# First attention layer of a four-layer transformer kernel: key tiles ahead of query tiles, square sums inside the next product, rope without GpSimd, and the first norm beside the modulation

## The chip, the cores and the metric

The kernel runs on one core of one Trainium2 chip. The metric is the device time of one execution in microseconds. The engines are called TensorE (PE in the profile), VectorE (DVE), ScalarE (ACT), GpSimd (POOL) and SyncE (SP, whose queue issues most loads). All numbers are f32.

## The reference, cut to what matters

Two blocks of two layers each work on 512 image tokens and 256 context tokens of width 1024. The change lies in layer 0, up to the first score of its attention:

```python
def rms_norm(x, g):
    y = xf * lax.rsqrt(jnp.mean(xf * xf, axis=-1, keepdims=True) + EPS)
    return (y * g.astype(jnp.float32)).astype(x.dtype)

mx = jnp.split(c_act @ ada_w[i] + ada_b[i], 6, axis=-1)   # modulation, mc from c_ctx
h_x = modulate(rms_norm(x, norm1_g[i]), mx[0], mx[1])     # h * (1 + scale) + shift
h_c = modulate(rms_norm(y_ctx, norm1_g[i]), mc[0], mc[1])
...
q_x, k_x, v_x = jnp.split(h_x @ w_qkv, [qd, qd + kvd], axis=-1)   # 16 q heads, 4 kv heads of 64
q_x = rope_2d(rms_norm(q_x.reshape(B, S, N_HEADS, HEAD_DIM), q_gain), tables)
k_x = rope_2d(rms_norm(k_x.reshape(B, S, N_KV_HEADS, HEAD_DIM), k_gain), tables)
k_c = rms_norm(k_c.reshape(B, L, N_KV_HEADS, HEAD_DIM), k_gain)
...
s_ctx = einsum(qb, k_c) * scale; s_loc = einsum(qb, kb) * scale   # then softmax and values
```

The other layers (feed-forward, retention, two layers with four mixers each) are computed by code that the change leaves as it is.

## The kernel before

**Tiling.** Activations lie transposed: 8 tiles of 128 features by T = 768 tokens (512 image, 256 context). Every f32 factor of a large product is split into a high part (fp32r) and a low part, the rest. A weight unit of 128x1024 is loaded into `WR`; ScalarE rounds it to `WH` (`refill`, L692) and VectorE subtracts to get `WL` (L1037). There are two buffers each, so unit u waits until product u-2 is over. `product` (L313 to L328) makes one output tile of 128 features: 8 input tiles times three products (WH with HH, WH with HL, WL with HH). `product_pair` makes two output tiles at once as the input tiles become ready.

**Order.** Each engine has a program written out by hand; `on(name, event)` is a semaphore wait, `on.up` its increment. No scheduler moves anything, so the code is the order of each engine.

**Start.** The modulation of layer 0 is twelve parts of 512 columns. A part is two loads of 1 MB (`ada`), eight small matmuls (`ada_sum`, L363) into PSUM, a ScalarE copy (`ada_copy`, L698) and a turn into columns (`ada_turn`, L370). Parts 0 to 3 come ahead of the first norm, through two buffers `AR0`. Then the squares of X are made on ScalarE in two buffers (`all_squares`, L708) and summed over the features by eight products with a matrix of 1/1024 (`mean_square`, L388). Then come root (L703, L705), two Newton steps (`newton`, L1082, L1083), and for each tile: a scaling on VectorE (L1108, L1111), scale and shift on ScalarE (L725 to L732), and the low part on VectorE (L1095, L1098).

**Query, key and value tiles.** `attention` makes 8 query tiles, then 2 key tiles, then the value rows. A tile goes through: product into PS[0] or PS[1]; raw copy and square on ScalarE (L785, L786); square sum over each head's 64 features on TensorE (L438); root and Newton steps; the gain (L1181); the rope on VectorE (half swap L1183, sine multiply L1184, addition L1191) with the cosine multiply on GpSimd (L1542), which writes into the square's buffer. TensorE's order is product n, modulation part 4+n, square sum n, turn, product n+1. A key tile is then split into high and low parts and copied to the other half of the partitions (`aK`, L806, L807, L1203, L1204), from one buffer `aKF`. The value rows (`product_rows`, L352) go to six PSUM banks and from there to `aV`. Last come mask loads, the stacking of the first block's queries (`stack`, L820, L1222) and the first score (L459).

## Time and profile before

| | us |
|---|---|
| three executions, median | 3689.19 |
| three executions, lowest and highest | 3688.1, 3695.85 |
| the profiled execution, in all | 3685.29 |
| its span from first to last instruction | 3684.0 |
| TensorE busy | 3449.4 (94%) |
| VectorE busy | 1743.7 (47%) |
| ScalarE busy | 1214.7 (33%) |
| GpSimd busy | 255.6 (7%) |
| mean granted clock of TensorE | 0.963 |
| first matmul of the product pair | 63.61 |
| first score of the attention | 235.49 |

A time in the profile is counted from the span's start. A row of the timeline gives start, length, engine, source line, operation, output and inputs; in brackets is how long the engine was idle before it and what it then got. The granted clock is a share of 2.4 GHz: 0.50 is 1.2 GHz.

### The profile page before, as it was taken

The numbers are of one execution on the slowest core, as the hardware profiler recorded it, in microseconds if no ns is written. First come the engines' busy times: TensorE is split into PE (matmuls) and PEld (weight loads), VectorE is DVE, ScalarE is ACT, GpSimd is POOL, SyncE is SP. The second block draws the span as 40 slices with busy tenths as digits, with TensorE's granted clock in tenths as the row PEclk, the third lists the DMA queues.
The fourth block names the chain that finished last, engine by engine and source line by source line (L and its number), as shares of the span: only waits on it lengthen the run. The fifth ranks groups of instructions, "written<-read, shape, count | busy, mean of one in ns | idle before, by whom it ended". The sixth has DMA issues, their size and how long they took to land.

```text
span 3684.0 us, 42824 instructions
## 1 busy us (share of the span) xinstructions
PE 3449.4 (94%) x17952; PEld 2782.0 (76%) x17952; DVE 1743.7 (47%) x2627; ACT 1214.7 (33%) x1696; POOL 255.6 (7%) x337
## 2 busy tenths in 40 slices
PE   6979989999989999998999999889999989979998
PEld 3767778888865756656888786578888878568886
DVE  3567454333343333426757425546535433644343
ACT  4357442112232221224222424442212233543232
POOL 0101100000100000001001100010000010010001
PEclk7989999999999999999999998899999999889999
DMA  5400033323221211113544210023323322012222
GB/s 204 182 26 2 30 115 126 120 92 126 82 69 35 94 48 58 65 41 139 192 149 173 98 58 29 12 87 127 133 84 126 105 86 81 12 46 97 97 97 86
DMA packets 87776, 334.24 MB, mean 91 GB/s; under 512 B 11168, under 2 KB 14240, under 8 KB 83744
## 3 DMA queue, kind: packets, MB, share of 16 engines
q1 hardware_dynamic: 66416, 252.85, 19.3%
q0 software_dynamic: 21168, 78.65, 6.4%
q8 instruction: 142, 2.33, 0.2%
q14 instruction: 50, 0.41, 0.0%
HBM read 329.37 MB, written 2.10 MB: 90 GB/s over the span
## 4 chain that ended last, share of the span: by engine, by line
PE 89%; DVE 4%; ACT 4%; issue 1%; DMA 1%; SPq 0%; POOL 0%; DVEq 0%; ACTq 0%
PE PS L326 65%; PE PS L352 6%; PE PS L548 3%; PE PS L521 2%; PE PS L339 2%; PE PS L620 1%; PE PS L470 1%; PE PS L513 1%; PE PS L483 1%; PE PS L645 1%; PE PS L459 1%; PE PS L591 1%; DMA AR<-in_ada 1%; PE PS L632 1%; DVE dP L1450 1%
## 5 line engine op out<-in xcount | busy, mean ns | idle before, releaser
L692 ACT ACTIVATE WH<-WR 128x1024 fp32r<-128x1024 f32 (+1 forms) x376 | 419.0, 1115 | 1686.8 <-PE PS L326 1448.1
L326 PE MATMUL PS<-HH,WH 128*128 128x512 f32 (+1 forms) x3120 | 944.5, 358 | 29.7 <-DVE HL L1427 11.0
L326 PE MATMUL PS<-HL,WH 128*128 128x512 f32 (+1 forms) x3120 | 936.9, 355 | 0.0
L326 PE MATMUL PS<-HH,WL 128*128 128x512 f32 (+1 forms) x3120 | 936.6, 355 | 0.0
L1037 DVE TENSOR_TENSOR WL<-WR,WH 128x1024 fp32r<-128x1024 f32 (+1 forms) x376 | 486.0, 1293 | 928.6 <-ACT WH L692 928.2
L326 PEld LDWEIGHTS PS<-HH,WH 128*128 128x128 f32 x3120 | 514.6, 189 | 122.4 <-issue 16.6
L326 PEld LDWEIGHTS PS<-HL,WH 128*128 128x128 f32 x3120 | 514.4, 189 | 88.0 <-issue 2.2
L326 PEld LDWEIGHTS PS<-HH,WL 128*128 128x128 f32 x3120 | 513.9, 189 | 86.6
L326 PE MATMUL PS<-DH,WL 128*128 128x512 f32 (+1 forms) x1056 | 318.7, 356 | 0.0
L326 PE MATMUL PS<-DL,WH 128*128 128x512 f32 (+1 forms) x1056 | 318.7, 356 | 0.0
L326 PE MATMUL PS<-DH,WH 128*128 128x512 f32 (+1 forms) x1056 | 318.6, 356 | 0.0
L1163 DVE SCALAR_TENSOR_TENSOR X<-PS,MOD,X 128x512 f32<-128x512 f32 x96 | 60.6, 659 | 368.0 <-PE PS L326 368.0
L326 PEld LDWEIGHTS PS<-DL,WH 128*128 128x128 f32 x1056 | 174.2, 188 | 30.0
L326 PEld LDWEIGHTS PS<-DH,WL 128*128 128x128 f32 x1056 | 174.2, 188 | 30.0
L326 PEld LDWEIGHTS PS<-DH,WH 128*128 128x128 f32 x1056 | 174.1, 188 | 30.0
L1068 DVE SCALAR_TENSOR_TENSOR PS<-AT,CB 128x1024 f32<-128x1024 f32 x144 | 176.5, 1226 | 0.0
L352 PE MATMUL PS<-WH,HH 128*128 128x256 f32 (+1 forms) x416 | 142.2, 342 | 27.5 <-DVE HL L1095 15.8
L1536 POOL DMA_DIRECT2D AT<-in_adat x144 | 76.0, 528 | 1149.5 <-DVE AT L1068 574.7
L352 PE MATMUL PS<-WL,HH 128*128 128x256 f32 (+1 forms) x416 | 141.0, 339 | 0.0
L352 PE MATMUL PS<-WH,HL 128*128 128x256 f32 (+1 forms) x416 | 141.0, 339 | 0.0
L1528 POOL TENSOR_TENSOR WK<-WK,WK 128x768 f32<-128x768 f32 (+1 forms) x56 | 116.9, 2087 | 329.3 <-ACT WK L708 328.8
L767 ACT ACTIVATE DH<-WK 128x768 fp32r<-128x768 f32 (+1 forms) x88 | 65.1, 739 | 185.4 <-DVE WK L1154 185.4
(258 smaller groups left out, 3707.1 us busy)
## 6 DMA issues: line engine op xcount, KB each, us to landing
WR<-in_win SPq DMA_DIRECT2D x176, 512.0 KB, 3.5
AT<-in_adat POOLq DMA_DIRECT2D x144, 512.0 KB, 3.8
WR<-in_wdn SPq DMA_DIRECT2D x64, 704.0 KB, 4.0
WR<-in_wret SPq DMA_DIRECT2D x64, 512.0 KB, 3.6
WR<-in_zin SPq DMA_DIRECT2D x36, 512.0 KB, 3.5
AR<-in_ada SPq DMA_DIRECT2D x8, 1024.0 KB, 4.9
aV<-in_ada SPq DMA_DIRECT2D x8, 1024.0 KB, 4.9
aAR<-in_ada SPq DMA_DIRECT2D x8, 1024.0 KB, 6.5
```

Source lines behind the costliest of these rows:

```text
L326: mm = PE.matmul(dst[:, a:b], w[u % 2][:, k * P:(k + 1) * P], h[:, k, a:b], start=(k == 0 and i == 0), stop=(k == nk - 1 and i == 2))
L339: mm = PE.matmul(dst[v][:, a:b], w[(u + v) % 2][:, k * P:(k + 1) * P], h[:, k, a:b], start=(k == 0 and i == 0), stop=(k == KT - 1 and i == 2))
L352: mm = PE.matmul(dst(m), h[:, k0 + k, m * P:(m + 1) * P], w[u % 2][:, k * width:(k + 1) * width], start=(first and k == 0 and i == 0 and n ...
L521: mm = PE.matmul(d, M.rV[:, m, e * P:(e + 1) * P], M.rAT[:, m, :], start=(m == 0), stop=(m == 5))
L548: mm = PE.matmul(PS[half][:, 512 * v:512 * v + 512], wt[half][:, col:col + P], y[:, k, :], start=(k == 0 and i == 0), stop=(k == 3 and i = ...
L692: AC.activation(M.WH[u % 2][:, 0:n], M.WR[u % 2][:, 0:n], COPY).then_inc(*on.up("w_hi", u))
L767: AC.activation(M.DH[:, j, 0:n], HF[:, 0:n], COPY).then_inc(*on.up("d_hi", (l, jj)))
L1037: VE.tensor_tensor(M.WL[u % 2][:, 0:n], M.WR[u % 2][:, 0:n], M.WH[u % 2][:, 0:n].bitcast(F32), ALU.subtract).then_inc(*on.up("w_lo", u))
L1068: i = VE.scalar_tensor_tensor((PS[3], M.AT[v % 3])[j][:, :], M.AT[v % 3][:, :], 1.0, M.CB[:, j, :], ALU.mult, ALU.mult, accum_out=MOD[:, l ...
L1163: i = VE.scalar_tensor_tensor(X[:, m, a:b], PS[m % 2 if m else 2][:, a:b], MOD[:, l, 40 + m, j:j + 1], X[:, m, a:b], ALU.mult, ALU.add)
L1528: PO.tensor_tensor(WK[2][:, 0:n], WK[2][:, 0:n], WK[k % 2][:, 0:n], ALU.add).then_inc(*on.up("square_summed", (tag, k)))
L1536: PO.dma_start(M.AT[v % 3][:, :], dram["adat"][l - 1, v]).then_inc(*on.up(f"mod_load{v % 3}", (l, v), 16))
```

## The change

- **Start.** `AR0` has four buffers, so parts 2 and 3 wait for the sums two parts back. ScalarE squares X between the copies of the modulation parts. GpSimd adds up seven of the eight squares (`squares`, the helper the later norms use); TensorE's mean square is two products and stands after the turn of part 2, ahead of part 3. VectorE does root, Newton steps and five scalings and then the modulation of parts 0 to 3 and the low parts of the first two weight units. The first tile of this norm takes the path of the others.
- **Order of tiles.** `QK = (8, 9, 0, ..., 7)`: keys first. The weight array is laid out in that order. The keys' rope result stands in the places of queries 6 and 7 until it is split, which happens after the tiles at places 3 and 4.
- **Inside the next product.** `product` calls `between(k)` ahead of each input tile. From place 2 on, the square sum of the tile before stands ahead of input tile 2 (3 in one case) and the turn ahead of input tile 5; the last one's stand inside the value rows.
- **ScalarE** takes the square of a tile after the Newton steps of the tile before.
- **Rope.** The cosine multiply is on VectorE, in place, and GpSimd has no part in it.
- **Values.** The rows go to three banks, two tiles to a bank; ScalarE copies a whole bank and VectorE none. The mask loads wait for the last rope, and `stack` comes before the last weight units.

```diff
 def first_ada(self):
-        self.AR0 = [t(f"AR0{i}", [P, 4, 512]) for i in range(2)]
+        self.AR0 = []
+        for i, at in enumerate(FIRST_ADA):
+            self.top = at
+            self.AR0.append(self.tile(f"AR0{i}", [P, 4, 512]))
...
+QK = (8, 9, 0, 1, 2, 3, 4, 5, 6, 7)
+V_PLACES = (0, 1, 2)
...
         for k in range(nk):
-            if between and k == 3:
-                between()
+            if between:
+                between(k)
...
     def attention():
         u = FIRST["qkv"]
-        for n in range(10):
-            half = n % 2
-            if n == 0:
-                product_pair(u, PS, ALL, ("h_lo", "0a"))
-            if n > 1:
-                product(u + n, PS[half], (HH, HL), KT, ALL, ("q_squared", n - 2))
-            if n < 8:
-                ada_sum(0, A0 + n, buf, (0, A0 + n - 1))
-            PE.wait_ge(*on("q_squared", n))
-            PE.wait_ge(*on("table", "attention") if n == 0 else on("rms", ("q", n - 1)))
+        def square_sum(p):
+            PE.wait_ge(*on("q_squared", QK[p]))
+            PE.wait_ge(*on("rms", ("q", QK[p - 1])) if p else on("table", "attention"))
...
+        def beside(p, at, squares_at, turn_at):
+            if at == squares_at and p != 1:
+                square_sum(p)
+            if at == turn_at and p > 1:
+                ada_turn(0, A0 + QK[p], M.aKF)
+        product_pair(u, PS, ALL, ("h_lo", "0a"))
+        for p in range(2, 10):
+            last = p - 1 if p > 2 else 0
+            product(u + p, PS[p % 2], (HH, HL), KT, ALL, ("q_squared", QK[p - 2]) if p > 3 else None, None,
+                    lambda k: beside(last, k, 3 if p == 3 else 2, 5))
+            if p == 2:
+                square_sum(1)
+            ada_sum(0, A0 + QK[p], buf, (0, A0 + QK[p] - 1))
...
     for nb in range(A0):
-        ada_sum(0, nb, M.AR0, before_part(0, nb))
+        ada_sum(0, nb, M.AR0[2 * (nb % 2):2 * (nb % 2) + 2], before_part(0, nb))
         ada_turn(0, nb, M.EV0)
-    mean_square("0a", ALL, False)
+        if nb == A0 - 2:
+            mean_square("0a", ALL)
...
-    for nb in range(A0):
-        ada_copy(0, nb, M.EV0[:, :])
+    ada_copy(0, 0, M.EV0[:, :])
+    AC.wait_ge(*on("x_load", 0))
+    squares("0a", T, range(4))
+    ada_copy(0, 1, M.EV0[:, :])
+    squares("0a", T, range(4, KT))
+    ada_copy(0, 2, M.EV0[:, :])
+    root("0a", T)
+    ada_copy(0, 3, M.EV0[:, :])
     refill(0)
     refill(1)
-    AC.wait_ge(*on("ada_turned", (0, A0 - 1)))
-    AC.wait_ge(*on("x_load", 0))
-    all_squares("0a", T)
     norm("0a", 0, 0, ALL)
...
+            if p:
+                AC.wait_ge(*on("rms", ("q", QK[p - 1])))
+            AC.activation(M.aSQ[:, :], PS[p % 2][:, 0:T], SQUARE).then_inc(*on.up("q_squared", n))
+            refill(u + p + 2)
...
+            if p in (3, 4):
+                key_high(p - 3)
...
+        AC.wait_ge(*on("rope", QK[-1]))
         for g in range(2):
             stack(0, g)
+        for v in range(2):
+            refill(u + 12 + v)
+        for i in range(3):
+            AC.wait_ge(*(on("v_rows", i) if i < 2 else on("product", u + 11)))
+            a = (2, 4, 0)[i]
+            AC.activation(flat(M.aV, a, a + 2), bank(PS, V_PLACES[i]), COPY).then_inc(*on.up("aV", i))
...
+            VE.tensor_tensor(raw[:, 0:S], raw[:, 0:S], M.aCOS[:, :], ALU.mult)
             step(VE.tensor_tensor(M.aT2[:, :], M.aT2[:, :], M.aSIN[:, :], ALU.mult), ("q_sin", n))
-            VE.wait_ge(*on("q_t1", n))
...
-        PO.wait_ge(*on("table", "attention"))
-        for n in range(10):
-            PO.wait_ge(*on("q_normed", n))
-            PO.tensor_tensor(M.aSQ[:, 0:S], M.aRAW[n % 2][:, 0:S], M.aCOS[:, :], ALU.mult).then_inc(*on.up("q_t1", n))
...
     for nb in range(1, A0):
         for half in range(2):
-            ada(0, nb, half, buf, (0, nb - 1))
+            ada(0, nb, half, buf[2 * (nb % 2):2 * (nb % 2) + 2], (0, nb - 2) if nb > 1 else None)
```

How TensorE's order moves in the start, in the kernel before, from the sum of part 3 (`AR`, `CAC`) to the mean squares (`WK`, `ONE`):

```order
L363 MATMUL PS<-AR_71,CAC 32x512 x4
L363 MATMUL PS<-AR_72,CAC 32x512 x4
L370 MATMUL PS<-SEL,EV_73 128x2 x4
L388 MATMUL PS<-WK_103,ONE 128x512
L388 MATMUL PS<-WK_103,ONE 128x256
L388 MATMUL PS<-WK_104,ONE 128x512
L388 MATMUL PS<-WK_104,ONE 128x256
```

And in the changed kernel, from the sum of part 2 to the product pair:

```order
L381 MATMUL PS<-AR_71,CAC 32x512 x4
L381 MATMUL PS<-AR_72,CAC 32x512 x4
L388 MATMUL PS<-SEL,EV_75 128x2 x4
L399 MATMUL PS<-WK_107,ONE 128x512
L399 MATMUL PS<-WK_107,ONE 128x256
L399 MATMUL PS<-WK_106,ONE 128x512
L399 MATMUL PS<-WK_106,ONE 128x256
L381 MATMUL PS<-AR_73,CAC 32x512 x4
L381 MATMUL PS<-AR_74,CAC 32x512 x4
L388 MATMUL PS<-SEL,EV_75 128x2 x4
L353 MATMUL PS<-HH,WH_55 128x512
```

The mean square has become two products (the sum `WK_107` and the last square `WK_106`) and stands ahead of part 3 instead of behind it.

TensorE after the product pair, before: the pair's last matmuls, then one modulation part (`aV`, `aAR`), the square sum of tile 0 (`aBD`) and the turn (`SEL`). The same five follow once more for tile 1, and then product 2 begins.

```order
L339 MATMUL PS1<-HH_50,WL1_58 128x512
L339 MATMUL PS1<-HH_50,WL1_58 128x256
L363 MATMUL PS3<-aV_76,CAC_61 32x512 x4
L363 MATMUL PS3<-aAR_87,CAC_61 32x512 x4
L438 MATMUL PS2<-aSQ_79,aBD_85 128x512
L438 MATMUL PS2<-aSQ_79,aBD_85 128x256
L370 MATMUL PS3<-SEL_65,aKF_82 128x2 x4
```

Now product 2 (`PS0`) follows the pair at once; this is the place inside it, ahead of its input tile 2:

```order
L340 MATMUL PS0<-HH_50,WL0_57 128x512
L340 MATMUL PS0<-HH_50,WL0_57 128x256
L441 MATMUL PS2<-aSQ_82,aBD_88 128x512
L441 MATMUL PS2<-aSQ_82,aBD_88 128x256
L340 MATMUL PS0<-HH_50,WH0_55 128x512
L340 MATMUL PS0<-HH_50,WH0_55 128x256
```

The first key's square sum stands between two input tiles of product 2. VectorE in one query tile's turn, before and after:

```order
L1037 TENSOR_TENSOR WL_57<-WR_53,WH_55 128x1024
L1082 SCALAR_TENSOR_TENSOR aSQ<-PS,aSQ 128x768
L1083 SCALAR_TENSOR_TENSOR aRI<-aSQ,aRI 128x768
L1181 SCALAR_TENSOR_TENSOR aR_77<-aR_77,aQG,aRI 128x768
L1183 STREAM_SHUFFLE aT_81<-aR_77 128x512
L1184 TENSOR_TENSOR aT_81<-aT_81,aSIN 128x512
L1191 TENSOR_TENSOR aQ<-aSQ,aT_81 128x512
```

```order
L1074 TENSOR_TENSOR WL_57<-WR_53,WH_55 128x1024
L1119 SCALAR_TENSOR_TENSOR aSQ<-PS,aSQ 128x768
L1120 SCALAR_TENSOR_TENSOR aRI<-aSQ,aRI 128x768
L1240 SCALAR_TENSOR_TENSOR aR_80<-aR_80,aQG,aRI 128x768
L1244 STREAM_SHUFFLE aT_84<-aR_80 128x512
L1245 TENSOR_TENSOR aR_80<-aR_80,aCOS 128x512
L1246 TENSOR_TENSOR aT_84<-aT_84,aSIN 128x512
L1251 TENSOR_TENSOR aQ<-aR_80,aT_84 128x512
```

VectorE has one instruction more, the cosine multiply at L1245.

## Rows read from the trace of the kernel before

**Rows 1.** Busy time by stretch: start:end, length, busy PE PEld DVE ACT POOL, PEclk, DMA.

```profile
82.70:99.10 16.40, 11.85 (x57) 5.12 (x57) 7.98 (x9) 8.01 (x11) 1.28 (x1) 0.69 0.82 312
99.10:182.70 83.60, 83.60 (x504) 62.98 (x505) 46.14 (x59) 31.94 (x45) 9.10 (x7) 1.00 0.45 172
182.70:206.40 23.70, 13.41 (x59) 9.41 (x58) 14.28 (x20) 12.98 (x19) 1.30 (x1) 0.81 0.14 45
206.40:226.10 19.70, 19.61 (x144) 19.41 (x144) 9.19 (x14) 5.66 (x10) 1.28 (x1) 0.88 0.00 1
196.00:198.00 2.00, 0.00 (x0) 0.00 (x0) 1.91 (x5) 1.90 (x5) 0.00 (x0) 0.88 0.00 0
```

**Rows 2.** TensorE's timeline in the start: start, length, line, operation, idle before it.

```profile
23.72 1.94 PE L363 MATMUL PS<-AR,CAC 128*32 128x512 f32 x8 [0.54 <-DMA AR<-in_ada]
...
40.12 1.87 PE L370 MATMUL PS<-SEL,EV 128*128 128x2 f32 x8 [0.72 <-ACT EV L698]
...
63.61 0.98 PE L339 MATMUL PS<-HH,WH 128*128 128x512 f32 x2 [7.92 <-DVE HL L1095]
```

**Rows 3.** The load of X: its issue, and its time to landing.

```profile
L1617 SPq DMA_DIRECT2D X<-in_xt x1: 432/432/432, 5.0 to 5.0; - x1
...
DMA to landing us min/median/max: 13.7/13.7/13.7
```

**Rows 4.** GpSimd's additions of squares in the later norms, ns min/median/max.

```profile
L1528 POOL TENSOR_TENSOR WK<-WK,WK x56: 1287/1990/2556, 417.6 to 3664.0; 128x768 f32<-128x768 f32 x35, 128x512 f32<-128x512 f32 x21
```

**Rows 5.** The chain of waits up to 262 us: start, length, engine and line.

```profile
55.73 0.91 ACT RI L703
...
59.52 1.15 DVE TT L1108 x2
...
63.61 19.09 PE PS L339 x96
...
145.47 1.85 PE PS L363 x16
147.32 1.49 PE PS L438 x4
148.81 0.79 PE PS L370 x8
149.59 8.43 PE PS L326 x48
```

**Rows 6.** VectorE's timeline in the start and after the pair.

```profile
42.67 2.36 DVE L1037 TENSOR_TENSOR WL<-WR,WH 128x1024 fp32r<-128x1024 f32 x2
...
60.58 1.82 DVE L1111 TENSOR_TENSOR TT<-X,RI 128x768 f32<-128x768 f32 x2
...
84.23 1.23 DVE L1037 TENSOR_TENSOR WL<-WR,WH 128x1024 fp32r<-128x1024 f32 x1 [6.89 <-ACT WH L692]
```

**Rows 7.** TensorE's timeline around the keys and at the first score.

```profile
184.75 1.56 PE L438 MATMUL PS<-aSQ,aBD 128*128 128x512 f32 x4 [1.60 <-ACT aSQ L786]
...
199.63 2.93 PE L438 MATMUL PS<-aSQ,aBD 128*128 128x512 f32 x4 [4.85 <-ACT aSQ L786]
...
235.49 0.98 PE L459 MATMUL PS<-aK,aQS 128*128 128x128 f32 x3 [9.46 <-DVE aQS L1222]
```

**Rows 8.** Groups of instructions from 99 to 182 us: busy us, mean ns, idle before.

```profile
L1542 POOL TENSOR_TENSOR aSQ<-aR,aCOS 128x512 f32<-128x512 f32 x7 | 9.1, 1300 | 78.7 <-DVE aR L1181 78.7
L1184 DVE TENSOR_TENSOR aT<-aT,aSIN 128x512 f32<-128x512 f32 x7 | 7.7, 1102 | 0.2
...
L692 ACT ACTIVATE WH<-WR 128x1024 fp32r<-128x1024 f32 x6 | 6.3, 1058 | 0.0
...
L1191 DVE TENSOR_TENSOR aQ<-aSQ,aT 128x512 f32<-128x512 f32 x7 | 4.8, 692 | 0.2
L786 ACT ACTIVATE aSQ<-PS 128x768 f32<-128x768 f32 x6 | 4.8, 807 | 0.0
...
L698 ACT ACTIVATE aKF<-PS 128x512 f32<-128x512 f32 x6 | 3.6, 598 | 0.0
```

**Rows 9.** Groups of instructions on ScalarE from 193 to 216 us, both key tiles.

```profile
L806 ACT ACTIVATE aK<-aKF 64x256 fp32r<-64x256 f32 (+1 forms) x8 | 4.2, 522 | 4.6 <-DVE aKF L1191 4.5
```

260 lines of the change are left out of this document (133 added, 127 removed).

## The prediction

> **What bounds the kernel now.** I read the busy time by stretch first, then TensorE's timeline and the chain of waits inside each stretch, then the groups of instructions with their mean times. The change touches only what lies before the first attention score, so a reader has to see how much of these 235.5 us TensorE does not work at full clock. In the turns from 99.1 to 182.7 us it is busy all the time at a granted clock of 1.00 [rows 1]; there the chain is TensorE alone, 1.85 us of modulation sum, 1.49 of square sum, a turn of 0.79 (the rest up to 149.59) and a product of 8.43, together 12.56 us [rows 5]. Nothing that is merely reordered inside such a turn can save anything. The loss is at the ends: 4.6 us idle at a clock of 0.69 after the product pair, 10.3 us idle at 0.81 around the two key tiles, clock 0.88 in the value rows [rows 1], and 9.5 us of waiting before the first score [rows 7]. Ahead of the pair, TensorE waits for loads, then the squares and the norm run one after the other until 63.61 [rows 2]. The rest of the program has no edit.
>
> I call E the end of the product pair, 82.70 before (63.61 + 19.09) [rows 5]. From E to the first score (235.5) are 152.8 us.
>
> **Part 1: first norm beside modulation.** Removed: the squares after the modulation. Added: seven GpSimd additions of 1.99 us [rows 4], two more load buffers, and two mean-square products of 128x768 in place of eight.
> - Loads. X is issued at 5.0 and lands 13.7 later, at 18.7 [rows 3]; the second part's halves are in by 23.7 [rows 2], 2.5 us for each 1 MB. With four buffers the queue of transfers does not run dry, so the third part is in by 28.7 and the fourth by 33.7. In the kernel before, the fourth part's turn came only at 40.1 to 42.0 [rows 2].
> - Squares: first at 18.7 + 0.8, then seven additions in a row, 13.9 us and some hand-offs: 33.8. The last square is at about 32.6 and holds ScalarE back, so the copy of the third part ends at 33.2 and its turn (1.87 [rows 2]) at 35.1. Then the mean squares: 2 x 1.49 = 3.0 at full clock, 6 at half. I take 5.2, as the engine starts slow, which gives 40.3 (38.1 to 41.1).
> - The root and the Newton steps took 55.73 to 59.52, 3.8 us [rows 5]: 44.1. Five scalings at 0.91 [rows 6]: 48.7. Meanwhile TensorE does the fourth sum (2 x 1.94), copy 0.6 [rows 8] and turn 1.87 even at half clock by 46.7, so that chain is not late. Modulation and its scale took from 42.0 to 42.67, 0.7 us; the two weight subtractions 2.36 [rows 6]; one low part 0.95. The pair starts at 52.8, or 53.6 with slow mean squares. I take 53.2 against 63.61: **10.4 us gained**, 9 to 12.5. What hid the two subtractions before was the wait for the squares; now they stand on the path, and the 2.4 us are in this sum.
>
> The pair then takes its 19.1 us as before: it starts at the slow clock again (two products at full clock would be 16.9), and the norm's steps for each tile, which feed it, are the same from the second tile on.
>
> **Part 2: keys first, squares and turns inside the next product.** Times from E. The work on TensorE does not change: eight turns of 12.56, two further square sums (3.0), and the value rows, 19.61 us at 0.88, so 17.3 at full clock [rows 1]; 120.8 in all. Before, 32 us of idle and slow clock came on top. After:
> - First tile. Its raw copy and square (0.81 each, of one shape), high part (1.06) [rows 8] and low part stay; in the trace of before the low part ends at 84.23 + 1.23, 2.8 us after E [rows 6]. Now TensorE waits for it with nothing to do: **2.8 us** idle. Product 2 then runs, the keys' square sum inside from 4.9 to 6.4.
> - Second tile. ScalarE takes its square only after the first has its Newton steps: 6.4 + 3.8 + 1.0 for the gain + 0.4 copy + 0.7 + 0.8 = 13.2. TensorE is there at 12.7: **0.6**.
> - Third tile. Modulation sum, product 3 from 16.8, its third tile at 19.9. VectorE must end the rope, do the low part (1.23) and the Newton steps of the second tile, and ScalarE then copies and squares: 21.8, **1.9**.
> - Turns 4 and 5 carry the keys' split: eight copies on ScalarE each, 4.2 us (sixteen copies in all, of which eight have 4.2 us [rows 9]), and eight subtractions on VectorE. The square sum comes 3.95 us after a product's end (sum 1.85 and two tiles), its input 1.6 after; the split pushes the input to 4.1: **0.2 each**. From then on the input is 2.3 us early, and the Newton steps end 9.3 us into a turn of 12.6.
> - End. The last rope is over at 13.6 us after product 9, its stacking by 17.5; the value rows end at 21.5 and cover both, and the mask loads too. What is left is one high part (1.06, queued ahead on ScalarE) and two copies of a bank, 0.5 to 0.6 each [rows 8]: **2.1** in place of 9.5 [rows 7].
>
> Idle sum 8.0. Two more switches per turn from product to something else and back, 0.09 each (24 matmul pairs at 0.347 are 8.32, the piece has 8.43 [rows 5]): 1.4 for eight turns, 0 to 2.
>
> The **clock** after E: TensorE fell idle at 194.8 (4.85 us before 199.63 [rows 7]) and the granted clock of 196 to 198 is 0.88 in the mean [rows 1], so it went from 2.4 to 1.2 GHz at about 197.5, after 2.7 us. Here the idle time is 2.8, right at that edge. A slow restart costs about 2.2 (19.09 against 16.86 for two products), and it lies on the path since the square sum waits behind it. I take it, 2.1; at the other bound 0. The Trainium skill, "TensorE: Matmul & The Clock Gate", section "What's actually happening", says that the length of the slow phase differs from run to run and should not be fitted; by it this term is no constant but a spread, and the sum would be 2 us more or less from one run to the next. The rows show both outcomes: after 1.60 us idle the square sum took 1.56, the full-clock length, and after 4.85 us the clock was down [rows 7].
>
> 120.8 + 8.0 + 1.4 + 2.1 = 132.3 against 152.8: **20.5 us gained**, 17 to 25.
>
> **Part 3: rope without GpSimd.** GpSimd's cosine multiply (1.30) runs beside VectorE's sine multiply, which takes 1.10 where the addition of the same shape takes 0.69 [rows 8]. With both on VectorE it is 0.69 + 0.69 in a row, 0.3 us longer up to the rope, and VectorE has that time: it is busy 46 of 83.6 us [rows 1]. On the path it is worth nothing, except at the third tile, where the 0.3 is in the walk above. The bound below is -1.
>
> **Sum.** 10.4 + 20.5 = 30.9 us. The profiled execution has 3684.0 us of span, 3685.3 in all; the median of the three runs is 3689.2, and I set the sum against that: 3658.3, said as **3658**. By the profiled execution it would be 3654.
>
> **The rivals.**
> - *The clock stays up* at E and again at the first score (the wait is 2.1, and both ends of a head step gain): 2.1 more, 1.5 at the scores, no cost of switches 1.4. 3653. For it: 2.8 is hardly more than the 2.7 for which the clock stayed. Against: it is more.
> - *The start gives little.* If GpSimd's additions take the 2.56 us that the longest of them took [rows 4], seven give 4 us more; if X or the third part lands 2 us later, that adds too. Gain 4 to 5 at the start: 3664. Against it: the median is 1.99, and VectorE, beside which the long ones could arise, has no work there.
> - *The key turns stall.* If the eight copies and the eight subtractions follow each other instead of overlapping, the two turns lose up to 4.2 each: 3667. Against it: each subtraction waits for its own copy alone.
> - *It does not do what it says*: the squares still stop the product because their input is late in every turn. Input 1.6, need 3.95; it would need 2.4 us more of delay in each of seven turns, and each further 1 us costs 7. With 3 us: 3663.
> - *Slower*: the weight loads. A unit's load is queued on SyncE behind two 1 MB modulation loads that wait for the sum of the part before. Issued some 3 us into a turn, it must be in 14.1 us into it (next product's end + 1.6), so it may take 10.9 us. The mean DMA share in the turns is 0.45 [rows 1], room for about twice. The decision point is 10.9 us; to come out slower by 0.2% all of seven turns would have to take 5.4 us longer, a landing of 16 us, over the 13.7 of the 3 MB transfer [rows 3]: 3700. The order and the amount are those of before, which speaks against it.
>
> **How the numbers follow.** Forecast with slow restart 0.50; clock stays up 0.20; start gives little 0.12; key turns or late squares 0.11; slower 0.02; the rest, things not seen, 0.05, half of it within 0.2%. Range 3645 to 3670: from the clock rival with a good start (3653 less 2, and less the 4 us by which the profiled execution lies under the median) to the key rival with its 3 us. A measurement of this kernel tells about 0.2% (7 us) from no change. Faster 0.94, same 0.03, slower 0.03.
>
> **What would show it.** First matmul of the pair at 52.8 to 53.6, with GpSimd's additions from about 19.6 to 33.8; the pair's end near 72.3; then idle of 2.8, 0.6 and 1.9 us and none over 0.3 until the value rows end; turns of 12.6 to 12.8; 2.1 us before the first score, which comes at 204 to 205 in place of 235.5. After it the distances are those of before. Wrong would be: a square sum that waits in each turn, a pair that starts after 58, a wait for a weight load, or a gain given back in a stage behind.

## The result and the profile after

| | before | after |
|---|---|---|
| executions of the comparison | 4 | 4 |
| median, us | 3689.3 | 3656.03 |
| lowest and highest, us | 3688.1, 3695.85 | 3651.22, 3660.02 |
| profiled execution, in all | 3685.29 | 3651.22 |
| its span | 3684.0 | 3649.9 |
| first matmul of the product pair | 63.61 | 50.35 |
| end of the pair (E) | 82.70 | 69.26 |
| first score | 235.49 | 199.50 |
| first product of the project stage, behind the attention | 406.69 | 369.93 |

The ratio of after to before is 0.9906, with an interval of 0.9889 to 0.9923: 33 us less. The forecast was 3658, with a range of 3645 to 3670.

The four longest waits of TensorE in the kernel after, from 40 to 205 us: who waited, for what, us in total, times, longest.

```profile
PE PS L353 <- DVE HL L1137: 8.6, 1, 8.6
PE PS L340 <- DVE WL L1074: 2.8, 1, 2.8
PE PS L478 <- ACT aV L859: 2.2, 1, 2.2
PE PS L441 <- ACT aSQ L829: 1.9, 2, 1.5
```

The first is the wait for the pair, the second the one for the third weight unit's low part, which stands on ScalarE and VectorE behind the eviction of the first tile. The square sums (L441) wait twice, 1.9 us together; before they waited 8.5 in three places, two of which are in [rows 7] (1.60 and 4.85). The wait of 9.46 before the first score [rows 7] has become 2.2. TensorE's timeline gives the places (start, length, line, operation, in brackets the idle time before):

```profile
32.73 1.05 PE L388 MATMUL PS<-SEL,EV 128*128 128x2 f32 x8 [1.29 <-ACT EV L721]
33.64 4.52 PE L399 MATMUL PS<-WK,ONE 128*128 128x512 f32 x8
...
50.35 0.98 PE L353 MATMUL PS<-HH,WH 128*128 128x512 f32 x2 [8.56 <-DVE HL L1137]
...
72.09 1.01 PE L340 MATMUL PS<-HH,WH 128*128 128x512 f32 x2 [2.83 <-DVE WL L1074]
...
83.92 1.56 PE L441 MATMUL PS<-aSQ,aBD 128*128 128x512 f32 x4 [0.40 <-ACT aSQ L829]
...
92.23 1.56 PE L441 MATMUL PS<-aSQ,aBD 128*128 128x512 f32 x4 [1.52 <-ACT aSQ L829]
...
199.50 1.58 PE L478 MATMUL PS<-aK,aQS 128*128 128x128 f32 x12 [2.18 <-ACT aV L859]
```

The stretches that answer to [rows 1], with the same columns: the first tile, the turns, and the value rows.

```profile
69.30:84.00 14.70, 11.51 (x53) 9.34 (x53) 6.06 (x8) 5.10 (x8) 0.00 (x0) 0.88 0.11 38
84.00:180.00 96.00, 94.48 (x571) 69.17 (x572) 65.78 (x91) 49.74 (x73) 0.00 (x0) 1.00 0.51 197
180.00:197.30 17.30, 17.30 (x139) 16.58 (x137) 9.87 (x15) 5.34 (x6) 0.00 (x0) 1.00 0.21 67
```

Where before 10.3 us of idle time lay around the two key tiles and the value rows ran at 0.88 [rows 1], TensorE now works from 84 to 197.3 us with 1.5 us of idle time, at a granted clock of 1.00. A turn in the chain of waits, to compare with 12.56 in [rows 5]:

```profile
112.59 1.85 PE PS L381 x16
...
116.75 1.29 PE PS L441 x4
...
121.22 0.79 PE PS L388 x8
...
125.23 1.85 PE PS L381 x16
```

From one modulation sum to the next (112.59 to 125.23) are 12.64 us; the next two intervals are 12.67 and 12.65 (137.90 and 150.55 are the next two starts). The product is in pieces, with the square sum and the turn between them, and the switches cost 0.1 per turn. The rope stands on VectorE alone (groups from 99 to 182 us: busy us, mean ns, idle before):

```profile
L1245 DVE TENSOR_TENSOR aR<-aR,aCOS 128x512 f32<-128x512 f32 x7 | 4.8, 692 | 0.2
...
L1246 DVE TENSOR_TENSOR aT<-aT,aSIN 128x512 f32<-128x512 f32 x7 | 4.8, 684 | 0.0
```

The sine multiply took 1.10 beside GpSimd [rows 8] and takes 0.68 without it.

The books: 13.3 us gained at the start of the pair, 36.0 at the first score, 36.8 at the project stage, 34.1 in the span. So 22.6 us lie between E and the first score (152.8 before, 130.2 after). Behind the project stage, where the code is the same, the kernel after took 2.7 us more (3280.0 against 3277.3); the experiments tell how much that means.

### The profile page after: what moved, and what is told of

The parts are those of the page before. It is cut to its first block, busy times and chain, and to the rows that moved or that the text cites. A ratio compares the mean times of both kernels' runs of the same rounds, so it can differ in the third digit from the quotient of the medians.

```text
span 3649.9 us, 42781 instructions
## 1 busy us (share of the span) xinstructions
PE 3433.7 (94%) x17928; PEld 2775.6 (76%) x17928; DVE 1743.7 (48%) x2632; ACT 1215.7 (33%) x1697; POOL 255.4 (7%) x335
## 4 chain that ended last, share of the span: by engine, by line
PE 89%; DVE 4%; ACT 4%; issue 1%; DMA 0%; POOL 0%; SPq 0%; DVEq 0%; ACTq 0%; POOLq 0%
PE PS L340 66%; PE PS L368 6%; PE PS L570 3%; PE PS L543 2%; PE PS L353 2%; PE PS L642 1%; PE PS L535 1%; PE PS L490 1%; PE PS L505 1%; PE PS L667 1%; PE PS L613 1%; PE PS L478 1%; PE PS L654 1%; DVE dP L1497 1%; ACT aPT L867 1%
## 5 line engine op out<-in xcount | busy, mean ns | idle before, releaser
L1578 POOL TENSOR_TENSOR WK<-WK,WK 128x768 f32<-128x768 f32 (+1 forms) x63 | 129.5, 2055 | 349.1 <-ACT WK L731 347.8
## 6 DMA issues: line engine op xcount, KB each, us to landing
AR<-in_ada SPq DMA_DIRECT2D x8, 1024.0 KB, 11.5
```

The source lines that it names most:

```text
L1578: PO.tensor_tensor(WK[2][:, 0:n], WK[2][:, 0:n], WK[k % 2][:, 0:n], ALU.add).then_inc(*on.up("square_summed", (tag, k)))
```

## The experiments

Each run is read by the same marks. From end_undone to warm each kernel ran once. P is the first matmul of the pair, E the pair's end (for the runs with a wait there, the start of what follows less the wait; for warm and best_warm, the start of the added products), S the first score. Each row is one profiled execution.

| kernel | P | E | S | S - E | span |
|---|---|---|---|---|---|
| before | 63.61 | 82.70 | 235.49 | 152.8 | 3684.0 |
| start_only | 52.14 | 71.80 | 225.39 | 153.6 | 3680.1 |
| tiles_only | 64.13 | 83.36 | 213.52 | 130.2 | 3674.6 |
| after | 50.35 | 69.26 | 199.50 | 130.2 | 3649.9 |
| after_again | 52.18 | 71.34 | 201.70 | 130.4 | 3652.4 |
| end_undone | 51.05 | 69.61 | 207.72 | 138.1 | 3667.4 |
| last_outside | 51.62 | 70.45 | 205.44 | 135.0 | 3654.5 |
| outside | 52.14 | 71.20 | 204.48 | 133.3 | 3655.5 |
| keys_last | 51.60 | 70.42 | 202.97 | 132.6 | 3651.5 |
| rope_pool | 50.47 | 69.90 | 204.84 | 134.9 | 3654.0 |
| two_buffers | 51.71 | 70.57 | 202.13 | 131.6 | 3650.6 |
| warm | 52.04 | 71.30 | 200.31 | 129.0 | 3652.2 |
| best | 51.92 | 70.96 | 196.27 | 125.3 | 3645.0 |
| best_warm | 51.91 | 70.76 | 196.20 | 125.4 | 3652.3 |

### The two halves apart

start_only is the kernel before with the start of the changed one (squares and mean square beside the modulation, four load buffers):

```diff
-    mean_square("0a", ALL, False)
+        if nb == A0 - 2:
+            mean_square("0a", ALL, True)
```

> The kernel before with the new start alone (four load buffers, squares between the modulation parts, first norm beside the modulation). My theory: the two halves of the change are independent and add. The product pair starts at 50.4 us as in the changed kernel, and from there to the first score everything is as before (171.9 us from 63.61 to 235.49), so the first score comes at 222 us and the total is 13 us under before: 3676. Rival: part of the start's gain is given back in the first tiles, because the loads of modulation part 4 and of the third weight unit come no earlier; then the first score is later than 224 and the total gains under 11.

tiles_only is the changed kernel with the start of the one before:

```diff
-        if nb == A0 - 2:
-            mean_square("0a", ALL)
+    mean_square("0a", ALL, False)
     attention()
```

> The changed kernel with the start put back as it was (two load buffers, squares behind the modulation, norm behind it). Theory: the pair starts at 63.6 as before, and from the pair's end to the first score it takes the changed kernel's 130.2 us instead of 152.8, so the first score comes at 213 and the total is 22 us under before: 3667. Rival: the two halves overlap in what they save (both remove idle time in front of the first tiles); then the first score is later than 216 here or later than 224 in the kernel with the start alone, and the two gains sum to clearly more or less than 34.

Measured: start_only 3673.71 us (ratio 0.9962, interval 0.9949 to 0.9975), tiles_only 3674.1 (0.9947, 0.9928 to 0.9966), beside 3690.43 for the kernel before. The two gains in the ratios, 0.38% and 0.53%, add up to 0.91%; the whole change has 0.94%. (The medians as they stand would give 0.45% and 0.44%, which adds up to much the same.) The traces are sharper than the times: S - E is 130.2 in tiles_only and in the kernel after to the tenth, and with the old tiles the new start is worth 11.5 us at P. At S the halves gain 10.1 and 22.0, together 32.1, where the whole change has 36.0 and its second execution, after_again, 33.8. Against after_again, whose pair started as late as that of start_only (52.18 and 52.14), the halves lack 1.7 us, most of it the 1.4 us that follow.

In start_only only 10.1 of the 11.5 reach the first score, which came at 225.4 and not at 222: that is the mark of my rival (later than 224), though the total gained 16.8 and not under 11. Part of the 1.4 us lost is one wait, for a modulation load. TensorE's waits in start_only:

```profile
PE PS L463 <- DVE aQS L1246: 9.1, 1, 9.1
...
PE PS L367 <- DMA aV<-in_ada: 2.9, 1, 2.9
```

The load of `aV` is waited for 2.0 us in the kernel before; with an earlier pair it is 2.9, since the load did not come earlier by as much. The wait at the first score is that of the kernel before, 9.1 for 9.5. The rest lies ahead of E: the pair took 19.66 us (52.14 to 71.80) in place of 19.09, and the granted clock read 0.50 up to about 57.6, 5.5 us into the pair, where in the kernel before it rose some 4.2 us into it.

### The end: stacking ahead of the value copies

end_undone stacks the queries behind the copies of the value rows again, and the mask loads wait for these copies:

```diff
-        AC.wait_ge(*on("rope", QK[-1]))
-        for g in range(2):
-            stack(0, g)
         for v in range(2):
             refill(u + 12 + v)
...
+        AC.wait_ge(*on("rope", QK[-1]))
+        for g in range(2):
+            stack(0, g)
...
+    SP.wait_ge(*on("aV", 2))
```

> The changed kernel with its last step put back: the mask loads and the stacking of the first block's queries come after the copies of the value rows, as in the kernel before, instead of under the value rows. Theory: the 7.3 us that went from the wait before the first score (9.46 to 2.18) are this step, so the wait is 8.5 to 9.5 us again and the first score comes at 206 to 207, 7 us after the changed kernel's 199.5. Rival: the wait was shortened by the three whole-bank copies in place of six; then the wait stays under 5 us.

```profile
PE PS L478 <- DVE aQS L1260: 8.6, 1, 8.6
```

The wait is 8.6, as expected; the first score came at 207.7, a little behind the 206 to 207. The wait is 6.4 us more than 2.2; S - E is 7.9 more, and most of the difference stands in the next view, TensorE's windows (length, busy, granted clock, DMA share, GB/s):

```profile
72.00:74.00 2.00, 1.56 (x5) 0.50 0.16 37
74.00:76.00 2.00, 2.00 (x8) 0.50 0.61 234
76.00:80.00 4.00, 4.00 (x14) 0.68 0.00 0
```

The slow phase behind the pair lasted until after 76 us in this execution: from E to the second tile's square sum it took 16.1 us, where the kernel after took 14.7. The edit lies far behind that place, and the matter returns below.

### Order of the tiles, and the place of the sums

keys_last takes the queries first and the keys last. The two keys are then split one after the other directly ahead of the value rows, through one buffer as in the kernel before, and the modulation's turns have a buffer of their own; the sums stay inside the next product. outside keeps the keys first but puts each square sum and each turn behind the product again. last_outside does both.

```diff
-QK = (8, 9, 0, 1, 2, 3, 4, 5, 6, 7)
+QK = (0, 1, 2, 3, 4, 5, 6, 7, 8, 9)
```

```diff
-            product(u + p, PS[p % 2], (HH, HL), KT, ALL, ("q_squared", QK[p - 2]) if p > 3 else None, None,
-                    lambda k: beside(last, k, 3 if p == 3 else 2, 5))
             if p == 2:
+                square_sum(0)
                 square_sum(1)
+            product(u + p, PS[p % 2], (HH, HL), KT, ALL, ("q_squared", QK[p - 2]) if p > 3 else None)
             ada_sum(0, A0 + QK[p], buf, (0, A0 + QK[p] - 1))
+            square_sum(p)
+            ada_turn(0, A0 + QK[p], M.aKF)
```

> The changed kernel with the keys last (queries 0 to 7, then keys) and with square sums and turns behind each product instead of inside the next one; start, rope on VectorE and the early stacking stay. This undoes both of the change's named steps at once. Theory: keys last with squares outside costs one wait of some 5 us at the second key (its square waits until ScalarE has split the first key) and 2 to 3 us at the first tiles; the value rows still cover the last rope and the second split. First score at 206 to 208, against 199.5. Rival (the change's own words, and my part 2): these two steps carry the gain of the key stretch and of the first tiles, 15 us or more; then the first score is at 214 or later.

> Edit: the changed kernel with the queries first and the two key tiles last, directly ahead of the value products; square sums and modulation turns stay inside the next product, as in the changed kernel. Measure: when TensorE's first score product starts (199.50 in the changed kernel). Theory (what counts is where the sums stand, the order of the tiles is worth next to nothing, because the value products cover the last tile's rope and split either way): 199.5 to 201, since the start of the queries' product waits no more than that of the keys. Rival (the keys' order is a part of the gain in its own right: keys split last leave the first scores waiting for the low parts of the last key): 205 to 210, with a wait of several us at the first score for VectorE or ScalarE in place of the 2.2 us for the copy of the values.

> Edit: the changed kernel with keys first, but with each square sum and each turn of the modulation behind the product at whose end it stands in the kernel before, and not some places into the next one. Together with the kernel that also had the keys last (first score 205.4, 5.9 us later than in the changed kernel, with waits of 0.6, 6.8 and about 2.5 us at the first three tiles) this tells how much of that is the place of the sums. Theory (the place is what counts, and nearly all of it at the first three tiles, where the pipeline fills): first score at 203 to 207, the waits at the tiles as in the kernel with the keys last. Rival (it was the order of the tiles): 199.5 to 201.

Measured S - E: 132.6, 133.3 and 135.0 against 130.2. The place of the sums costs 3.1 us and the order 2.4, together 4.8. TensorE's waits up to 205 us in outside, then in last_outside:

```profile
PE PS L441 <- ACT aSQ L831: 7.3, 2, 6.8
```

```profile
PE PS L447 <- ACT aSQ L837: 9.8, 3, 6.8
```

(The expectation for last_outside had 206 to 208, and its rival 214 or later; it came at 205.4.) With the sums behind the product the second tile's is waited for 6.8 us, with nothing to do meanwhile, where the changed kernel puts product 2. In exchange the 2.8 us behind the pair go, since the first square sum, which waits only 0.56 us, stands there, and the third tile does not wait at all. That is how 6.8 us of stall cost only 3.1. In the steady turns none of these kernels waits: from 100 to 175 us TensorE is busy throughout. The third wait of last_outside, which I had put at the third tile when I wrote the expectation for outside, is 2.45 us at 183.28, at the last key. So moving the sums is a matter of the first three tiles.

The order came out otherwise than my theory had it: 2.4 us and not 0 to 1.5, though far from the rival's 5 to 10. Its place is one wait of TensorE in keys_last, and ScalarE's timeline ahead of it shows the cause:

```profile
183.26 1.56 PE L447 MATMUL PS<-aSQ,aBD 128*128 128x512 f32 x4 [2.11 <-ACT aSQ L835]
```

```profile
177.47 0.42 ACT L824 ACTIVATE aK<-aKF 64x256 fp32r<-64x256 f32 x1 [2.42 <-DVE aKF L1257]
...
181.19 0.63 ACT L825 ACTIVATE aK<-aKF 64x512 fp32r<-64x512 f32 x1
181.72 0.79 ACT L832 ACTIVATE aR<-PS 128x768 f32<-128x768 f32 x1
182.41 0.79 ACT L835 ACTIVATE aSQ<-PS 128x768 f32<-128x768 f32 x1
```

The eight copies of the first key (177.47 to 181.72) stand in ScalarE's queue ahead of the second key's raw copy and square. In the changed kernel the split follows two tiles later, where nobody waits for it. The first score itself waits 2.2 us in both, so the wait that the rival had put there did not come.

### The rope

rope_pool gives the cosine multiply back to GpSimd, through the buffer of the squares as before; so a tile's square waits for the whole rope of the tile before.

```diff
-                AC.wait_ge(*on("rms", ("q", QK[p - 1])))
+                AC.wait_ge(*on("rope", QK[p - 1]))
...
-            VE.tensor_tensor(raw[:, 0:S], raw[:, 0:S], M.aCOS[:, :], ALU.mult)
             step(VE.tensor_tensor(M.aT2[:, :], M.aT2[:, :], M.aSIN[:, :], ALU.mult), ("q_sin", n))
+            VE.wait_ge(*on("q_t1", n))
...
+            PO.tensor_tensor(M.aSQ[:, 0:S], M.aRAW[p % 2][:, 0:S], M.aCOS[:, :], ALU.mult).then_inc(*on.up("q_t1", n))
```

> Edit: the changed kernel with the rope's multiplication by the cosines back on GpSimd, which writes it into the buffer of the squares, so that ScalarE's next square waits for the whole rope of the tile before. Theory of the document (the rope on VectorE alone is worth something only where the pipeline fills, at the first three tiles, and nothing in the steady turns, where both engines have slack): first score 1 to 4 us later than 199.50, all of it ahead of 100 us; no wait at the square sums of the later tiles. Rival A (it is worth nothing): within 0.5 us. Rival B (the chain through GpSimd binds every turn): 0.5 us or more at each of ten turns, first score over 204.5.

```profile
86.28 2.93 PE L441 MATMUL PS<-aSQ,aBD 128*128 128x512 f32 x4 [2.10 <-ACT aSQ L829]
...
97.59 1.56 PE L441 MATMUL PS<-aSQ,aBD 128*128 128x512 f32 x4 [2.96 <-ACT aSQ L829]
```

S - E is 134.9, 4.7 us more. The waits are 5.1 us in place of 1.9, and the first of them came with a low clock (0.50 from 87 to 89 us), at which the square sum took 2.93 in place of 1.56. From 100 to 175 us TensorE is busy for all 75. So the mechanism is the theory's (the first tiles, none of the steady turns), and its size is above the 1 to 4 us that I had given it. The first score came at 204.84, beyond the mark of rival B (204.5), but there is no wait in each turn, which is what rival B meant.

The run puts back two things at once, GpSimd and the shared buffer. Which of them costs is seen in the second tile, VectorE's addition that ends the first tile's rope and the square that ScalarE makes behind it:

```profile
84.70 0.69 DVE L1251 TENSOR_TENSOR aQ<-aSQ,aT 128x512 f32<-128x512 f32 x1
85.42 0.81 ACT L829 ACTIVATE aSQ<-PS 128x768 f32<-128x768 f32 x1 [1.59 <-DVE aQ L1251]
```

The raw copy ahead of it was over at 83.8, so this square stood 1.6 us waiting for the rope. GpSimd did not make the rope longer: from the first Newton step to the end of the rope are 5.7 us here (79.67 to 85.39) and 5.8 in the changed kernel (79.02 to 84.85). By these rows what costs is the shared buffer. A kernel with GpSimd and a buffer of its own for the cosine product was not run.

### The start: buffers, clock and what is on the path

two_buffers is the changed kernel with two load buffers at the start:

```diff
-        ada_sum(0, nb, M.AR0[2 * (nb % 2):2 * (nb % 2) + 2], before_part(0, nb))
+        ada_sum(0, nb, M.AR0[0:2], before_part(0, nb))
...
-            ada(0, nb, half, buf[2 * (nb % 2):2 * (nb % 2) + 2], (0, nb - 2) if nb > 1 else None)
+            ada(0, nb, half, buf[0:2], (0, nb - 1))
```

> Edit: the changed kernel with two load buffers for the modulation's halves at the start, in place of the four: each later half is again issued only when TensorE has summed the half before it in that buffer. Theory (the doubled buffers carry a part of the start's gain): the pair of products starts 1.5 to 3 us later than the changed kernel's 50.35 to 52.1. Rival (the loads are bound by the transfers themselves, the mean squares wait for the squares and not for the modulation): within 0.5 us of that range.

It started the pair at 51.71, inside the range of the changed kernel. The theory falls, and the rival's mark is met. Its turn of part 2 came at 33.32, where the eleven others with the new start have it at 32.67 to 32.96, so the two further buffers are worth 0.4 to 0.65 us.

after_again is the changed kernel, unedited:

> Edit: none; the changed kernel itself, beside the improved one, on the same chip. Expected by all theories: 3651 to 3661 us as before. Its profile tells by how much one stretch differs between two executions of the same code: seven executions with the new start began the first pair of products at 50.35 to 52.14 us. Theory (this spread comes from the clock that was granted while the mean squares and the turn behind them ran, at 32 to 36 us): the start of the pair is 50.3 to 50.6 if the turn of the modulation at about 32.7 us takes 1.05 us, and 51.6 to 52.2 if it takes 1.87. Rival (it comes from the transfers): a start of the pair that does not go with the turn's duration.

It took 3653.34 us (ratio 0.9909, 0.9895 to 0.9924), with P at 52.18 after a turn of 1.87, as the theory has it. TensorE's timeline in after_again, then in best:

```profile
32.80 1.87 PE L388 MATMUL PS<-SEL,EV 128*128 128x2 f32 x8 [0.84 <-ACT EV L721]
34.53 5.47 PE L399 MATMUL PS<-WK,ONE 128*128 128x512 f32 x8
```

```profile
32.71 1.87 PE L388 MATMUL PS<-SEL,EV 128*128 128x2 f32 x8 [0.83 <-ACT EV L721]
34.44 5.35 PE L399 MATMUL PS<-WK,ONE 128*128 128x512 f32 x8
```

The pair starts 12.2 us behind the end of the mean squares in each of the executions: 38.16 and 50.35 in after, 40.00 and 52.18 in after_again, 38.87 and 51.05 in end_undone, 39.79 and 51.92 in best. What spreads by 1.8 us is the turn (1.05 or 1.87) and the mean squares (4.4 to 5.5). For the mean squares the granted clock goes with it in most executions: 4.4 to 4.5 where it reads 1.00 up to 34 us, 4.9 to 5.5 where it reads 0.50 then. But in best and best_warm it reads 1.00 from 26 to 42 us and they took 5.35 and 5.33, and the turn took 1.87 at a reading of 1.00 in end_undone, two_buffers, best and best_warm. Nor does the turn alone give P, as the theory had put it: end_undone had a turn of 1.87 and started at 51.05, outside both of the theory's ranges, since its mean squares took only 4.37. So P goes with the turn and the mean squares together; the clock as their only cause is not shown, and what else sets them stays open.

### The clock behind the pair

warm puts ten products of a constant into the 2.8 us of waiting; nobody reads their result.

```diff
             last = p - 1 if p > 2 else 0
+            if p == 2:
+                for i in range(10):
+                    mm = PE.matmul(PS[2][:, 768:896], M.ONE[:, :], M.ONE[:, :], start=True, stop=True)
```

> Edit: the changed kernel with ten extra 128x128 products of a constant, whose result nobody reads, directly behind the first two tiles' products, in the 2.8 us in which TensorE waits there for the evicted first tile (69.3 to 72.1 us). In the changed kernel the granted clock fell to 0.50 at 72 to 74 us, after that wait, and was back at 1.00 from 76. Theory (the idle time is what lets the clock fall): the clock stays near 1.00 from 70 to 80 us and the first score comes 1.3 to 2.1 us earlier than 199.50. Rival (the clock falls whatever TensorE does there, as a consequence of what it did before): 0.50 in that stretch as before, and the first score within 0.3 us or later by what the ten products take.

TensorE's windows in the kernel after, and in warm:

```profile
72.00:74.00 2.00, 1.91 (x6) 0.50 0.39 104
74.00:76.00 2.00, 2.00 (x9) 0.69 0.42 166
76.00:80.00 4.00, 4.00 (x21) 1.00 0.00 0
```

```profile
72.00:74.00 2.00, 1.69 (x16) 1.00 0.00 0
74.00:76.00 2.00, 1.73 (x9) 1.00 0.41 43
76.00:80.00 4.00, 4.00 (x21) 1.00 0.28 110
```

The clock stays at 1.00, where it fell in each of the executions that had the 2.8 us of idle time. So the idle time is what lets it fall here. S - E is 129.0, 1.2 us less, a little under what I expected. (S itself came at 200.31, later than 199.50, because P was at 52.04.)

### A faster version

best shortens three waits: the low parts of the first two weight units ahead of the root and Newton steps (a), the third weight unit's rounding ahead of the first tile's raw copy (b), and the value copies ahead of the rounding of the last weight unit (c).

```diff
-            product(u + p, PS[p % 2], (HH, HL), KT, ALL, ("q_squared", QK[p - 2]) if p > 3 else None, None,
+            product(u + p, PS[p % 2], (HH, HL), KT, ALL, ("q_squared", QK[p - 2]) if p != 3 else None, None,
...
+    refill(0)
+    refill(1)
     root("0a", T)
     ada_copy(0, 3, M.EV0[:, :])
-    refill(0)
-    refill(1)
...
+            if p == 0:
+                refill(u + 2)
...
-        for v in range(2):
-            refill(u + 12 + v)
+        refill(u + 12)
...
+            if step == 6:
+                refill(u + 13)
```

> Edit: the changed kernel with three waits of its trace shortened. (a) The rounded high and low parts of the first two weight units are made ahead of the first norm's root and Newton steps, not behind them. (b) ScalarE rounds the third weight unit before it copies the first tile, which TensorE waits 2.83 us for. (c) The copies of the value products come before the rounding of the last weight unit, for which TensorE waits 2.18 us at the first score. Theory: (a) takes the 2.36 us of the low parts off the chain to the first product, (b) takes 1.1 us off the wait behind the first pair and may keep the clock from falling there (up to 1.7 us more), (c) takes 1 to 2 us off the wait at the first score; first score 4.5 to 6 us earlier than in the changed kernel, and the time 4 to 7 us under the changed kernel's in the same call. Rival (each of these waits is only handed to the next in line: the scalings of the first tiles, the squares, the stacking of the queries): within 2 us.

It took 3645.24 us, ratio 0.9891 with an interval of 0.9876 to 0.9905, beside 3653.34 and 0.9895 to 0.9924 for the changed kernel in the same comparison. The intervals overlap; the trace is clearer: S - E is 125.3, 4.9 us less. (The first score came 5.4 us earlier than in after_again and 3.2 earlier than in after, where 4.5 to 6 was expected; the time is 8.1 less, where 4 to 7 was.) (b) and (c) do it:

```profile
72.64 0.59 PE L340 MATMUL PS<-HH,WH 128*128 128x512 f32 x2 [1.68 <-ACT aSQ L831]
...
196.27 3.50 PE L478 MATMUL PS<-aK,aQS 128*128 128x128 f32 x24
```

The wait behind the pair is 1.68 in place of 2.83, and the first matmuls after it take 0.59 and not 1.01: the clock did not fall. What is left of the wait is for another engine's work than before: product 2 writes where the first tile lay, and must now wait until ScalarE has squared that tile, since the weight's rounding goes first (the first line of the edit adds this wait). Up to the second tile's square sum the edit makes 2.6 us (83.01 - 70.96 = 12.05, against 83.92 - 69.26 = 14.66). The first score waits for nothing.

(a) gave nothing at all. The chain of waits in the kernel after, and in best:

```profile
46.70 0.04 DVE SCL L1094
...
46.98 2.36 DVE WL L1074 x2
49.34 0.88 DVE HL L1137
...
50.35 17.87 PE PS L353 x90
```

```profile
48.54 1.31 ACT TT L757 x2
49.87 0.85 ACT HH L761
...
50.82 0.97 DVE HL L1141
```

ScalarE beside it, in the kernel after:

```profile
46.98 1.31 ACT L757 ACTIVATE TT<-TT,MOD,SCL 128x512 f32<-128x512 f32 x2 [4.41 <-DVE SCL L1094]
48.32 0.84 ACT L761 ACTIVATE HH<-TT 128x768 fp32r<-128x768 f32 x1
```

The chain of the kernel after goes through the two subtractions, which end at 49.34. With them gone, it goes through ScalarE's scale and shift (1.31) and rounding (0.85) of the first tile, which had run beside them all the time and ended at 49.16, almost as late. From the end of the mean squares to P are 12.19 us in the one (38.16 to 50.35) and 12.13 in the other (39.79 to 51.92).

best_warm adds products of a constant ahead of the pair and behind it:

```diff
+        for i in range(14):
+            PE.matmul(PS[0][:, 0:128], M.ONE[:, :], M.ONE[:, :], start=True, stop=True)
         product_pair(u, PS, ALL, ("h_lo", "0a"))
...
+            if p == 2:
+                for i in range(6):
+                    PE.matmul(PS[2][:, 768:896], M.ONE[:, :], M.ONE[:, :], start=True, stop=True)
```

> Edit: the improved kernel with extra 128x128 products of a constant, whose result nobody reads: 14 directly ahead of the first pair of products and 6 behind it, in the idle time of TensorE there. (In the changed kernel ten of them in the 2.8 us behind the pair kept the clock at 1.00 and brought the first score from 149.2 us behind the start of the pair to 148.3.) Theory (the clock at the start of the pair, 0.50 to 0.92 in its first 4 us, costs about 2 us, and filling the wait of some 6 us ahead of it gives them back): the pair takes 17 us in place of 18.9, and the first score comes 1.5 to 2.5 us earlier than in the improved kernel. Rival (the extra products run at the low clock themselves and end behind the wait, or the clock does not rise for them): no gain, or up to 2 us later.

The first score came at 196.20, 0.07 earlier than in best. That is the rival's outcome, though not for its reason: the fourteen products ran at a granted clock of 1.00, but they ended 5.3 us ahead of the pair, and the clock had fallen again by then, to 0.50 at 50 to 52 us. Whether more of them would help was not tried.

What this run shows instead is how far two executions can part in code that is the same. The first product of the project stage in best, then in best_warm:

```profile
366.77 0.64 PE L340 MATMUL PS<-HH,WH 128*128 128x512 f32 x2 [1.42 <-DVE HL L1306]
```

```profile
366.69 0.63 PE L340 MATMUL PS<-HH,WH 128*128 128x512 f32 x2 [1.42 <-DVE HL L1311]
```

The spans are 3645.0 and 3652.3. From that product to the end, identical code took 3278.2 and 3285.6; in before 3277.3, in after 3280.0, in after_again 3280.4, in start_only 3283.5 and in tiles_only 3289.6. In the two profiled executions this is why tiles_only is 22.0 us ahead of the kernel before at the first score and 9.4 at the end; that its median is ahead by 16 and not by 22 fits the same spread, but the other executions have no trace. My estimate from these rows is that a median can't be read to better than some 5 us, a mark to one or two.

## Why the prediction was right, and where it was not

**The result** lies 2 us from the forecast, 3656 against 3658. That is partly luck, since the single times spread by more (3651 to 3660). At the first score, whose place spreads by 2 us, the gain is 36.0 us for 30.9 forecast, 34 in after_again: it came at 199.5 and 201.7, where I had said 204 to 205. The start and the tiles each gave some 2 us more than forecast, and the time kept less of the gain than the mark did.

**The start** was forecast at 10.4 us, with P at 52.8 to 53.6. It is 50.35 and 52.18 in two executions of the same code, 11.4 to 13.3 us. The steps: X landed at 18.8 as taken from [rows 3], and the seven additions ran from 19.7 to 33.3, at 1.81 us each and not the 1.99 of [rows 4]. The mean squares took 4.5 (5.5 in after_again) for 5.2. From their end to the pair are 12.2, where my steps give 12.5 to 52.8 and I took 12.9.

What held the start was what I had said: the turn of part 2 waits for ScalarE's copy, which stands behind the last square, and that behind GpSimd's additions (the chain of waits goes through six of the seven). The step that was wrong in kind is the one on the weight subtractions: "now they stand on the path, and the 2.4 us are in this sum". The sum came out about right all the same, since ScalarE's 2.16 us for the first tile, which I had left out of it, take their place to the tenth when they go. I had followed one of two chains that meet at the low part of the first tile. The two further load buffers are worth some 0.5 us of the start's gain.

**From E to the first score** 132.3 was forecast and 130.2 measured. (The idle times of the walk add up to 7.8 and not to the 8.0 of the sum.) The idle times by the walk: 2.8 forecast and 2.83 measured behind the pair; 0.6 and 0.40; 1.9 and 1.52; 0.2 each and nothing at the keys' turns; 2.1 and 2.18 at the end. The switches cost 0.10 a turn in place of 0.18, 0.6 us less over the eight. The waits stand where the walk had them and for what it had them.

**The clock**: the slow restart, which I took as the likelier outcome of an idle time at the edge, came. By the stretch from E to the second tile's square sum it cost 1.5 us in after: 14.66 less the wait of 2.83 are 11.83, and in best, at full clock, 12.05 less 1.68 are 10.37. I had 2.1. In two_buffers, with the same wait of 2.82, the stretch was 16.0 and the cost 2.8, as the low clock lasted beyond 78 us. The Trainium skill says, in "TensorE: Matmul & The Clock Gate", section "What's actually happening", that the length of the slow phase is no constant from one run to the next; these executions agree. The other half of my rival on the clock, 1.5 us at the scores when it stays up there too, is neither shown nor refuted. In best the clock reads 1.00 from 196 to 215 us, in after 0.50 at 202 to 204, and yet both take the same from the first score to the project stage (170.5 and 170.4 us). But inside the softmax (L490) TensorE waits 16.0 us in all in best and 14.6 in after, so what the clock gave may have gone into these waits.

**The rope** I priced at nothing on the path, with a bound of -1. Given back to GpSimd and to the squares' buffer it costs 4.7 us. The step that failed is the one that looked at the engines and at the steady turns alone: there it is indeed nothing. But the cosine product had gone into the squares' buffer, and so the next square waits for the whole rope; where the pipeline fills, at the second and third tile, nothing covers that. By the rows of rope_pool it is the free buffer that is worth something, not the engine. In the forecast the error did not show, since the walk of these tiles was made with the new rope.

**The rivals.** TensorE waited for no weight load up to the first score in any run. The key turns did not stall; the eight copies of a key do cost 2.1 us of wait when they stand right ahead of the next tile's square, as keys_last shows, and the change put them where they don't. The squares are not late in the steady turns. A start that gives little did not come: the additions took 1.81 us, none 2.56. The rival of a slower kernel was priced a little high: seven turns of 5.4 us on 3658 make 3696 and not 3700.

**The parts together**: of the 36 us at the first score 11 to 13 are the start and 22.6 the tiles. Of the 22.6, the end's stacking has some 6.4, the rope's move with its buffer 4.7, the place of the sums 3.1 and the order 2.4 when each is undone alone. That is 16.6; the other 6 us are not assigned by any run. They may lie in steps that no run undid alone (the three banks for the values, the place of the squares) or in steps that cover each other.

## What to carry to other kernels

Where two chains of near equal length meet at one instruction, the chain of waits names one, and taking work off it gives nothing; look at what the waiting engine's other input did before pricing an edit (here 2.36 us of subtractions that were worth 0.06, since ScalarE's chain of 2.16 us beside them ended 0.2 us earlier). An engine taken out of a chain may also free a buffer, and that can be the larger part: here the buffer of the squares, whose late release cost the first tiles 4.7 us. An edit that is worth nothing in a steady turn can be worth several us where the pipeline fills and drains, so walk the first three tiles and the last one by themselves. And read a small change at a mark in the trace near its place: the same code differed by 12 us between executions over the rest of this program, and from the start of the pair to the first score the two executions of the changed kernel differ by 0.4 us (149.15 and 149.52).

## What was not expected of the hardware

- Behind the pair, idle time of 2.83 us let the clock fall to 0.50 (72 to 74 us in after). With 1.68 us in best, and with the wait filled by ten small products in warm, it stayed at 1.00. Keeping it was worth 1.2 us in warm. The length of the idle time does not settle it by itself: behind 2.10 us in rope_pool (at 86.28) the clock read 0.50 and the square sum took 2.93, behind 2.11 in keys_last and 2.45 in last_outside (both at 183.3) it read 1.00 and the square sum took 1.56.
- The same eight 128x2 products took 1.05 or 1.87 us, and the same mean squares 4.4 to 5.5, and the granted clock does not tell them apart in each execution: with a reading of 1.00 throughout they took 1.87 and 5.35 in best, 1.87 and 4.37 in end_undone.
- A 128x512 multiply on VectorE takes 0.68 us when GpSimd is silent and took 1.10 beside a GpSimd multiply of 1.30 [rows 8]. Doing both on VectorE (0.69 + 0.68) costs VectorE 0.27 us more than sharing them did.
